# The last layer norm of a 1-core encoder step: three scaling tiles move from ScalarE to GpSimd, and the output leaves in three transfers

## The chip, the cores and the metric

One core of a Trainium2 chip runs the whole program: TensorE (PE), VectorE (DVE), ScalarE (ACT), GpSimd (POOL) and SyncE (SP), which here only issues transfers and waits. The metric is the device time of one execution in microseconds. The kernel before was run three times: 957.76, 958.23 and 964.26, median 958.23 us.

## The reference, cut to what matters

The model is a two-layer hybrid encoder step on 256 prompt frames and 32 sample frames of 1024 features. Each layer is a mixer (RWKV-7, then forgetting attention), a layer norm, a mixture of experts and a second layer norm. The change touches only the very last of these four layer norms, whose result is the output y:

```python
def _layer_norm(z, g, b):
    zf = z.astype(F32)
    mu = jnp.mean(zf, -1, keepdims=True)
    var = jnp.mean(jnp.square(zf - mu), -1, keepdims=True)
    return ((zf - mu) * lax.rsqrt(var + LN_EPS) * g + b).astype(z.dtype)
...
        y = _hmoe(h, p['rg_w'][l], p['rg_b'][l], p['re_w'][l], p['re_b'][l],
                  p['exp_wg'][l], p['exp_wu'][l], p['exp_wd'][l])
        x = _layer_norm(ALPHA * x + gt2 * y, p['ln_g'][l, 1], p['ln_b'][l, 1])
```

## The kernel before, in words

Activations are held feature-major: the 1024 features are KT = 8 tiles of 128 partitions, and the 288 frames (T) lie along the free side, so that one tile is 128x288 float32 and the whole activation 128x2304, 1152 KB. X is the activation that a layer norm writes, Z the one that it reads and changes in place.

A layer norm (n = 0 to 3, the last is n = 3) is written once for each engine, in one function `layer_norm(n)` per engine, and the order on each engine is the order of the code. ACT squares the tiles (L2118) and POOL sums the squares (L2368) while the expert output is still being gathered; PE forms mean and variance (L989 to L996); ACT copies the mean (L2120). Then the mean is taken off: DVE does tiles 0 to 4 (L1617), POOL tiles 5 to 7 (L2373; OWN = 5). DVE works out the inverse of the variance (L1626 to L1628), ACT its root (L2124), DVE multiplies tile after tile by it (L1638, semaphore `u_ready`), and in the odd layer norms ACT follows with one instruction a tile that multiplies by g and adds b (L2128, semaphore `x_ready`). In the even layer norms POOL does that step for X (L2381), after a smaller job on the 32 sample frames of each tile (L2378, semaphore `hs_ready`). In n = 3 POOL has nothing after L2373.

SP, whose queue is in the order of its code, waits for all `x_ready` counts and then issues one transfer of X to the output (L678), waits for it to land, and then for the other outputs, which landed long before. Nothing else follows.

Of the kernel before, what the change touches and what calls it, by code (L numbers as in the profile page):

```python
# [12 lines left out]
ALU = mybir.AluOpType  # L13
# [4 lines left out]
D, KT = 1024, 8  # L18
TP, TS = 256, 32
T = TP + TS  # L20
# [37 lines left out]

MEAN_BANK, BONUS_BANK, VAR_BANK = (1, 2, 5), (6, 3, 4), (7, 0)
H0 = KT  # L60


VEC = {n: i * KT for i, n in enumerate(
# [183 lines left out]
def build(nc, I, O):  # L247
    ctx = ExitStack()
    with ctx:
# [3 lines left out]
        def sem(name):  # L253
            return ctx.enter_context(nc.semaphore(name))
# [31 lines left out]
        def cut(a, n):  # L286
            assert a + n <= ARENA, (a, n, ARENA)
            return arena[:, a:a + n]

        def act_flat(i):  # L290
            return cut(i * ACOL, ACOL)

        def acts(i):
            return act_flat(i).rearrange("p (k t) -> p k t", k=KT)

        A_X, A_H, A_KK, A_XX, A_B = 0, 1, 1, 2, 2
        A_R, A_K, A_V, A_G, A_LD, A_CUM, A_Y, A_A = 3, 4, 5, 6, 7, 8, 9, 10
        X, Hh = acts(A_X), acts(A_H)
# [16 lines left out]
        def v(name, k):  # L315
            return vec[:, VEC[name] + k:VEC[name] + k + 1]
# [6 lines left out]
        def folded(layer, what, k, stream):  # L323
            c = ((layer * 2 + what) * KT + k) * 2 + stream
            return fold[:, c:c + 1]
# [146 lines left out]
        s = {n: sem(n) for n in names}  # L472
# [45 lines left out]
        def _(sp):  # L518
# [155 lines left out]
            half(7, 0)  # L674
            sp.wait_ge(s["ada_done"], ADA_SLOTS)
            moe_loads(1)
            sp.wait_ge(s["x_ready"], 4 * KT)
            sp.dma_start(O["y"], act_flat(A_X)).then_inc(s["out_done"], 16)  # L678
            sp.wait_ge(s["out_done"], 16)
            sp.wait_ge(s["o_over"], 4)  # L680

            sp.wait_ge(s["shift_out"], 16)
# [6 lines left out]
        def _(pe):  # L689
# [10 lines left out]
            def project(mi, rhs_at, ready=None, then=None, first=0):  # L700

                for j in range(first, 2):
                    pe.wait_ge(wready[j], 16 * (mi + 1))
                    for o in range(4):
                        tile = 4 * j + o
                        if mi or tile >= 4:
                            pe.wait_ge(s["tile_free"], mi * 8 + tile - 3)
                        for k in range(KT):
                            if ready and tile == 0:
                                ready(k)  # L710
                            last = mm(ps[:, tile % 4, 0:T], wslot[j][:, k, o * P:(o + 1) * P], rhs_at(k),  # L711
                                      start=k == 0, stop=k == KT - 1)
                        last.then_inc(s["tile_done"], 1)
                        if then:
                            then(tile)
# [283 lines left out]
            def moe(layer):  # L999
# [3 lines left out]
                for k in range(KT):  # L1003
                    pe.wait_ge(s["h_ready"], H0 + 2 * KT * layer + k + 1)
                    pe.wait_ge(s["hs_ready"], KT * layer + k + 1)
# [213 lines left out]
            last.then_inc(s["f_mm"], 1)  # L1219
            pe.wait_ge(s["h_ready"], H0 + 2 * KT)  # L1220
            project(5, lambda k: Hh[:, k, :])
# [764 lines left out]
        def _(act):  # L1986
# [112 lines left out]
            for i in range(KT + 2):  # L2099
# [3 lines left out]
                k = i - 2  # L2103
# [8 lines left out]
            def layer_norm(n):  # L2112
                Z, layer = acts(ZB[n]), n // 2
                if n % 2:
                    act.wait_ge(s["o_over"], n + 1)
                for k in range(KT):
                    act.wait_ge(s["z_ready"], KT * n + k + 1)
                    Ac(acts(SQB[n])[:, k, :], Z[:, k, :], ACT.Square).then_inc(s["ln_sq"], 1)  # L2118
                act.wait_ge(s["ln_mean"], n + 1)
                Ac(lnmu, ps[:, 4, 0:T], ACT.Copy).then_inc(s["ln_mu"], 1)  # L2120
                act.wait_ge(s["ln_mu"], n + 1)
                Ac(lnm2, lnmu, ACT.Square).then_inc(s["ln_m2"], 1)
                act.wait_ge(s["ln_inv"], n + 1)
                Ac(lnr, lnr, ACT.Sqrt).then_inc(s["ln_rstd"], 1)  # L2124
                for k in range(KT):
                    act.wait_ge(s["u_ready"], KT * n + k + 1)
                    if n % 2:
                        Ac(X[:, k, :], Z[:, k, :], ACT.Identity, scale=v(f"g{layer}1", k), bias=v(f"b{layer}1", k))\  # L2128
                            .then_inc(s["x_ready"], 1)
                    else:  # L2130

                        Ac(Hh[:, k, 0:TP], Z[:, k, 0:TP], ACT.Identity, scale=folded(layer, 0, k, 0),
                           bias=folded(layer, 1, k, 0)).then_inc(s["h_ready"], 1)

            def moe(layer):
# [56 lines left out]
                for n in range(2):  # L2192
                    act.wait_ge(s["dn_mm"], layer * NDOWN + NPAIR + n)
                    Ac(ysel[1][:, n * 512:(n + 1) * 512], ps[:, 4 + n, :], ACT.Copy).then_inc(s["y_last"], 1)

            layer_norm(0)
            moe(0)
            layer_norm(1)

            def between(k):  # L2200
# [79 lines left out]
            act.dma_start(O["v"], act_flat(A_VO)).then_inc(s["kv_out"], 16)  # L2280
            act.wait_ge(s["kv_out"], 32)
            layer_norm(2)
            moe(1)
            layer_norm(3)
# [3 lines left out]
        def _(pool):  # L2288
            Pl = nc.gpsimd
# [66 lines left out]
            def layer_norm(n):  # L2356
                Z, Q, layer = acts(ZB[n]), acts(SQB[n]), n // 2
                if n % 2:
                    pool.wait_ge(s["z_in0"], 48 * (layer + 1))
                    for q in range(2):  # L2360
                        c = slice(q * 256, (q + 1) * 256)
                        ch.did(Pl.tensor_tensor(zin[:, 0:2, 0, c], zin[:, 0:2, 0, c], zin[:, 0:2, 1, c], ALU.add))
                        ch.link(Pl.tensor_tensor(zin[0:TS, 2, 0, c], zin[0:TS, 2, 0, c], zin[0:TS, 2, 1, c], ALU.add))
                        pool.sem_inc(s["zsum"], 1)

                for k in range(1, KT - 1):
                    pool.wait_ge(s["ln_sq"], KT * n + k + 1)
                    ch.link(Pl.tensor_tensor(ssum, Q[:, 0, :] if k == 1 else ssum, Q[:, k, :], ALU.add))  # L2368
                pool.sem_inc(s["ln_ssum"], 1)
                pool.wait_ge(s["ln_mu"], n + 1)  # L2370
                pool.wait_ge(s["ln_sq"], KT * (n + 1))
                for k in range(OWN, KT):
                    Pl.tensor_tensor(Z[:, k, :], Z[:, k, :], lnmu, ALU.subtract).then_inc(s["ln_cent"], 1)  # L2373
                if n % 2:
                    return
                for k in range(KT):
                    pool.wait_ge(s["u_ready"], KT * n + k + 1)
                    Pl.tensor_scalar(Hh[:, k, TP:T], Z[:, k, TP:T], folded(layer, 0, k, 1), folded(layer, 1, k, 1),  # L2378
                                     ALU.mult, ALU.add).then_inc(s["hs_ready"], 1)
                for k in range(KT):  # L2380
                    Pl.tensor_scalar(X[:, k, :], Z[:, k, :], v(f"g{layer}0", k), v(f"b{layer}0", k), ALU.mult, ALU.add)\  # L2381
                        .then_inc(s["x_ready"], 1)

            def moe(layer):
# [90 lines left out]
                for b in range(2):  # L2475
                    pool.wait_ge(s[f"o_gath{b}"], (np_ + base) * 16 + 16 * (layer + 1))
                    pool.sem_inc(s["o_over"], 1)

            layer_norm(0)
            moe(0)  # L2480
            layer_norm(1)

            pool.wait_ge(s["ada_done"], 4 * ADA_TURN)
            Pl.dma_start(clf[0:16, :], I["clf"]).then_inc(s["attn_small"], 16)
            for g in range(NGRP):
                if g >= 2:
                    pool.wait_ge(s["att_mm"], APE_TURN.after(g - 2, "SO"))
                for dst, src in ((CK, "ck"), (CV, "cv")):
                    Pl.dma_start(dst[g % 2], I[src][g]).then_inc(s[f"g_in{g % 2}"], 16)
            layer_norm(2)  # L2490
            moe(1)
            layer_norm(3)
# [137 lines left out]
```

## Time and profile before

| | us |
|---|---|
| median of three runs | 958.23 |
| the profiled execution's own time | 957.23 |
| its span, first to last instruction | 955.6 |

| engine | busy in the span |
|---|---|
| PE | 876.6 us, 92% |
| DVE | 368.9 us, 39% |
| ACT | 234.5 us, 25% |
| POOL | 185.4 us, 19% |

The shares are averages over the whole program. The mean granted clock of TensorE was 0.973 of full speed. The profile has a page of groups of instructions, a timeline in order of time (start, duration, engine, line, operation, and in brackets the idle time before it with what ended it), windows with the busy time of each engine and the DMA rate, and the chain of waits that ended last. In a timeline row "x6" after the shapes means that six instructions in a row are merged, and the duration is that of the whole group.

### The profile page before, as it was taken

To read this page: it belongs to the slowest core of one execution; us is meant where nothing else is said; L and a number is where in the kernel's file an instruction comes from. 1 tells how busy PE (TensorE), PEld (TensorE's weight loads), DVE (VectorE), ACT (ScalarE), POOL (GpSimd) and SP (SyncE) were. 2 spreads that over 40 slices of the span, in tenths; PEclk is the share of its full clock that TensorE was granted. 3 is DMA by queue.
4 is the path that set the end of the run, shared out by engine and by line. 5 is a ranking of instruction groups with operands and counts; after the bars stand their busy time and mean duration, and the time that the engine had idled before them with its cause. 6 is when DMAs were issued, how large, how long until landed. Compare 5 with 4: busy or idle time off the path is not lost.

```text
span 955.6 us, 19128 instructions
## 1 busy us (share of the span) xinstructions
PE 876.6 (92%) x8194; PEld 607.2 (64%) x8194; DVE 368.9 (39%) x869; ACT 234.5 (25%) x532; POOL 185.4 (19%) x237
## 2 busy tenths in 40 slices
PE   3899999989989999899988999999999998999873
PEld 0677667869987676655444567756567766554442
DVE  0614332536443647421221606933221374222226
ACT  0312224323322415111100415133232141111004
POOL 0100001203190225412131310000000244221213
PEclk9899999999999999799998999999999998999997
DMA  9947320432045965399999987334736744999941
GB/s 365 415 146 280 124 88 12 152 118 92 21 163 192 374 264 216 131 401 414 399 425 392 381 326 317 117 148 153 263 162 254 312 194 157 408 410 414 425 147 50
DMA packets 29877, 234.64 MB, mean 246 GB/s; under 512 B 6438, under 2 KB 6982, under 8 KB 14656
## 3 DMA queue, kind: packets, MB, share of 16 engines
q1 hardware_dynamic: 20736, 211.50, 55.3%
q0 software_dynamic: 8592, 19.52, 5.4%
q10 hardware_dynamic: 464, 2.39, 0.7%
q8 instruction: 65, 1.06, 0.4%
q14 instruction: 20, 0.16, 0.1%
HBM read 223.36 MB, written 18.94 MB: 254 GB/s over the span
## 4 chain that ended last, share of the span: by engine, by line
PE 76%; DMA 9%; DVE 6%; issue 4%; ACT 2%; POOL 1%; another core or an unknown queue 1%; SPq 0%; POOLq 0%; DVEq 0%; ACTq 0%
PE ps L711 22%; PE ps L1064 9%; PE ps L849 7%; PE ps L1111 5%; PE ps L693 4%; PE ps L856 3%; PE ps L732 3%; PE ps L1261 3%; DMA arena<-in_experts 3%; DMA arena<-in_w 2%; PE ps L1042 2%; PE ps L803 2%; PE ps L862 2%; PE ps L1156 1%; PE ps L774 1%
## 5 line engine op out<-in xcount | busy, mean ns | idle before, releaser
L711 PE MATMUL ps<-arena,ring 128*128 128x288 f32 x832 | 208.8, 411 | 3.8 <-ACT arena L2128 2.0
L711 PEld LDWEIGHTS ps<-arena,ring 128*128 128x128 f32 x832 | 157.4, 191 | 55.0 <-issue 8.7
L1064 PE MATMUL ps<-arena 128*64 128x256 f32 x960 | 118.3, 390 | 14.8 <-DMA arena<-in_experts 8.7
L1064 PEld LDWEIGHTS ps<-arena 128*64 128x64 f32 x960 | 68.0, 139 | 56.1 <-issue 15.1
L693 PEld LDWEIGHTS ps<-con,arena 128*128 128x128 f32 (+2 forms) x350 | 42.6, 148 | 38.0 <-issue 25.5
L849 PE MATMUL ps<-arena 64*64 64x64 f32 x1888 | 61.9, 219 | 5.2 <-issue 3.6
L693 PE MATMUL ps<-con,arena 128*128 128x128 f32 (+2 forms) x350 | 59.4, 302 | 6.7 <-DVE arena L1788 2.8
L849 PEld LDWEIGHTS ps<-arena 64*64 64x64 f32 x1888 | 58.8, 135 | 10.2 <-issue 6.7
L2157 ACT ACTIVATE arena<-ps 128x128 f32<-128x128 f32 x36 | 10.0, 278 | 196.8 <-PE ps L1064 183.5
L1111 PE MATMUL ps<-arena 128*64 128x512 f32 x176 | 51.0, 598 | 0.8 <-DVE arena L1791 0.8
L2021 ACT ACTIVATE arena<-ps 128x288 f32<-128x288 f32 x40 | 16.2, 408 | 121.6 <-PE ps L711 110.2
L2085 ACT ACTIVATE arena<-ps 128x512 f32<-128x512 f32 x44 | 26.2, 596 | 75.6 <-PE ps L849 55.1
L732 PE MATMUL ps<-arena,csil 128*32 128x512 f32 x192 | 26.9, 687 | 17.1 <-DMA arena<-in_w 17.1
L1602 DVE SCALAR_TENSOR_TENSOR arena<-ps,mod,arena 128x256 f32<-128x256 f32 x64 | 20.5, 361 | 52.5 <-PE ps L711 36.8
L1788 DVE TENSOR_TENSOR arena<-arena,ps 128x128 f32<-128x128 f32 x36 | 10.4, 288 | 76.2 <-ACT arena L2157 71.1
L1424 DVE SCALAR_TENSOR_TENSOR arena<-arena,vec 128x288 f32<-128x288 f32 x48 | 21.6, 513 | 42.6 <-PE ps L711 41.6
L1795 DVE TENSOR_SCALAR arena<-ps,TBL 128x512 f32<-128x512 f32 x24 | 16.9, 746 | 47.6 <-PE ps L1111 47.6
L2400 POOL DMA_INDIRECT arena<-hbuf,TBL x16 | 16.7, 1044 | 85.3 <-DVEq L1730 56.9
L1884 DVE SCALAR_TENSOR_TENSOR arena<-arena,csil 128x2048 f32<-128x2048 f32 x14 | 32.9, 2352 | 0.7
L1261 PE MATMUL ps<-arena,ring 128*128 128x288 f32 x128 | 32.7, 409 | 0.0
L2118 ACT ACTIVATE arena<-arena 128x288 f32<-128x288 f32 x32 | 14.2, 443 | 73.3 <-DVEq L1606 66.9
L698 PE MATMUL ps<-con 128*128 128x288 f32 x110 | 31.6, 441 | 0.0
(325 smaller groups left out, 1308.3 us busy)
## 6 DMA issues: line engine op xcount, KB each, us to landing
arena<-in_experts SPq DMA_DIRECT2D x30, 2048.0 KB, 13.2
ring<-in_w SPq DMA_DIRECT2D x24, 2048.0 KB, 8.6
arena<-in_w SPq DMA_DIRECT2D x16, 2048.0 KB, 13.3
arena<-in_experts SPq DMA_DIRECT2D x26, 1024.0 KB, 14.0
ring<-in_experts SPq DMA_DIRECT2D x6, 2048.0 KB, 10.5
ring<-in_experts SPq DMA_DIRECT2D x10, 1024.0 KB, 20.1
zbuf<-arena POOLq DMA_DIRECT2D x2, 2304.0 KB, 17.8
arena<-zbuf SPq DMA_DIRECT2D x8, 512.0 KB, 7.1
```

What stands on the lines that cost most here:

```text
L693: return nc.tensor.transpose(out, in_, ident[0:n, 0:n])
L698: mm(ps[:, bank, 0:T], ident, con[:, 0:T], start=True, stop=True)
L711: last = mm(ps[:, tile % 4, 0:T], wslot[j][:, k, o * P:(o + 1) * P], rhs_at(k), start=k == 0, stop=k == KT - 1)
L732: last = mm(ps[32 * q:32 * q + 32, ADA_BANK[turn], :], c2[:, 2 * j + k, :], w[:, k, q, :], start=j == 0 and k == 0, stop=j == ADA_TURN - 1 ...
L849: last = mm(o, lhs[r, k, :], rhs[r, k, :], start=True, stop=True)
L856: last = mm(ps[r, bank, k * 64:(k + 1) * 64], lhs[r, k, :], rhs[r, k, :], start=n == 0, stop=n == len(terms) - 1)
L1064: last = mm(ps[64 * j:64 * j + 64, 2 + b, 0:256], x(k), ewgu[slot][:, k, j * 256:(j + 1) * 256], start=k == 0, stop=k == KT - 1)
L1111: last = mm(ps[HALF[b], 4 + n, :], hidT[b][:, f * C:(f + 1) * C], ewd[dslot(2 * p + b)][:, f, n * 512:(n + 1) * 512], start=f == 0, stop=f ...
L1261: last = mm(ps[:, b, 0:T], wslot[j][:, k, o * P:(o + 1) * P], X[:, k, :], start=k == 0, stop=k == KT - 1)
L1424: last = V.scalar_tensor_tensor(cut((11 + n % 3) * ACOL + k * T, T), XX[:, k, :], v(f"mu{i}", k), Hh[:, k, :], ALU.mult, ALU.add)
L1884: link(V.scalar_tensor_tensor(turn5[st], w[:, k, :], x, turn5[st], ALU.mult, ALU.add))
L2085: ins = Ac(B[dst], src, ACT.Copy, scale=-1.0 if product == "Bt" else 1.0)
```

## The change

In the last layer norm, tiles 3, 5 and 7 get their multiplication by g and addition of b on POOL instead of ACT. ACT still waits for each tile's `u_ready`, and passes over these three. POOL signals them by `hs_ready`, ACT its five by `x_ready`. SP issues three transfers in place of one: tiles 0 to 2, tiles 3 to 5, tiles 6 and 7, each behind waits for its own tiles, and at the end waits for all three to land. (There are eight tiles; the words "nine tiles" that came with the change do not fit the code.)

```diff
+LAST_POOL = (3, 5, 7)
+LAST_OUT = ((0, 3), (3, 6), (6, 8))
...
             moe_loads(1)
-            sp.wait_ge(s["x_ready"], 4 * KT)
-            sp.dma_start(O["y"], act_flat(A_X)).then_inc(s["out_done"], 16)
-            sp.wait_ge(s["out_done"], 16)
+            for a, b in LAST_OUT:
+                if any(k in LAST_POOL for k in range(a, b)):
+                    sp.wait_ge(s["hs_ready"], 2 * KT + sum(k < b for k in LAST_POOL))
+                sp.wait_ge(s["x_ready"], 3 * KT + sum(k not in LAST_POOL for k in range(b)))
+                sp.dma_start(O["y"][:, a * T:b * T], act_flat(A_X)[:, a * T:b * T]).then_inc(s["out_done"], 16)
+            sp.wait_ge(s["out_done"], 16 * len(LAST_OUT))
...
                 for k in range(KT):
                     act.wait_ge(s["u_ready"], KT * n + k + 1)
+                    if n == 3 and k in LAST_POOL:
+                        continue
                     if n % 2:
                         Ac(X[:, k, :], Z[:, k, :], ACT.Identity, scale=v(f"g{layer}1", k), bias=v(f"b{layer}1", k))\
                             .then_inc(s["x_ready"], 1)
...
                 for k in range(OWN, KT):
                     Pl.tensor_tensor(Z[:, k, :], Z[:, k, :], lnmu, ALU.subtract).then_inc(s["ln_cent"], 1)
+                if n == 3:
+                    for k in LAST_POOL:
+                        pool.wait_ge(s["u_ready"], KT * n + k + 1)
+                        Pl.tensor_scalar(X[:, k, :], Z[:, k, :], v("g11", k), v("b11", k), ALU.mult, ALU.add)\
+                            .then_inc(s["hs_ready"], 1)
                 if n % 2:
                     return
```

On SP, at the end of its queue, before: the readback of the expert output, the one transfer of y, and the waits for the outputs.

```order
L507 DMA arena<-zbuf 128x2x512 [waits z_scat1,z_scat0]
L507 DMA arena<-zbuf 128x2x512
L507 DMA arena<-zbuf 32x2x512
L507 DMA arena<-zbuf 128x2x512 x2
L678 DMA out_y<-arena 128x2304 [waits x_ready]
L249 UNCONDITIONAL_BRANCH [waits st_out,kv_out,shift_out,logf_out,o_over,out_done]
```

The same place in the changed kernel (its line numbers are 3 to 13 higher):

```order
L510 DMA arena<-zbuf 128x2x512 x2
L510 DMA arena<-zbuf 32x2x512
L684 DMA out_y<-arena 128x864 [waits x_ready]
L684 DMA out_y<-arena 128x864 [waits x_ready,hs_ready]
L684 DMA out_y<-arena 128x576 [waits x_ready,hs_ready]
L252 UNCONDITIONAL_BRANCH [waits st_out,kv_out,shift_out,logf_out,o_over,out_done]
```

One transfer of 1152 KB became two of 432 KB and one of 288 KB, in one queue, each behind the waits of its tiles.

On POOL, at the end of its queue, the changed kernel has:

```order
L2376 TENSOR_TENSOR lnw<-arena 128x288 [waits pool_ch,ln_sq]
L2376 TENSOR_TENSOR lnw<-lnw,arena 128x288 [waits ln_sq,pool_ch] x5
L2381 TENSOR_TENSOR arena<-arena,lnw 128x288 [waits pool_ch,ln_sq,ln_mu]
L2381 TENSOR_TENSOR arena<-arena,lnw 128x288 x2
L2385 TENSOR_SCALAR arena<-arena,vec 128x288 [waits u_ready] x3
```

Only the last of these rows is new; the kernel before ends with the subtractions. On ACT the eight instructions of the last step became five: before

```order
L2122 ACTIVATE lnw<-lnw 128x288 [waits ln_mu]
L2124 ACT_TABLE_LOAD
L2124 ACTIVATE lnw<-lnw 128x288 [waits ln_inv]
L2128 ACTIVATE arena<-arena,vec 128x288 [waits u_ready] x8
L249 UNCONDITIONAL_BRANCH
```

and in the changed kernel

```order
L2128 ACTIVATE lnw<-lnw 128x288 [waits ln_mu]
L2130 ACT_TABLE_LOAD
L2130 ACTIVATE lnw<-lnw 128x288 [waits ln_inv]
L2136 ACTIVATE arena<-arena,vec 128x288 [waits u_ready] x5
L252 UNCONDITIONAL_BRANCH [waits u_ready]
```

The instructions of PE and DVE and their waits are the same in both kernels.

## Rows read from the trace of the kernel before

**Rows 1.** Chain of waits that ended last, end of the span: start, us, what.
```profile
939.86 0.77 PE ps L991 x2
...
943.37 1.96 DVE lnw L1628
945.34 0.02 issue
945.36 0.45 ACT lnw L2124
...
947.80 2.18 ACT arena L2128 x4
949.98 0.52 ACTq L249
950.50 0.52 ACT arena L2128
```

**Rows 2.** Timeline, last layer norm, after the root: DVE, ACT and SP.
```profile
946.33 4.69 ACT L2128 ACTIVATE arena<-arena,vec 128x288 f32<-128x288 f32 x8 [0.53 <-DVE arena L1638]
...
947.32 2.29 DVE L1638 TENSOR_TENSOR arena<-arena,lnw 128x288 f32<-128x288 f32 x6
951.04 0.36 SPq L678 DMA_DIRECT2D out_y<-arena  x1
```

**Rows 3.** Timeline of the same stretch in short windows: single instructions of DVE and ACT.
```profile
947.07 0.63 ACT L2128 ACTIVATE arena<-arena,vec 128x288 f32<-128x288 f32 x1
...
947.80 0.63 ACT L2128 ACTIVATE arena<-arena,vec 128x288 f32<-128x288 f32 x1
...
949.16 0.45 DVE L1638 TENSOR_TENSOR arena<-arena,lnw 128x288 f32<-128x288 f32 x1
```

**Rows 4.** Windows: start:end, length, engines, PE clock, DMA share, GB/s.
```profile
951.00:952.00 1.00, 0.00 (x0) 0.00 (x0) 0.00 (x0) 0.02 (x1) 0.00 (x0) 0.50 0.28 120
952.00:953.00 1.00, 0.00 (x0) 0.00 (x0) 0.00 (x0) 0.00 (x0) 0.00 (x0) 0.50 0.98 415
953.00:954.00 1.00, 0.00 (x0) 0.00 (x0) 0.00 (x0) 0.00 (x0) 0.00 (x0) 0.50 0.97 406
954.00:955.00 1.00, 0.00 (x0) 0.00 (x0) 0.00 (x0) 0.00 (x0) 0.00 (x0) 0.50 0.57 240
```

**Rows 5.** DMA issues: what, queue, count, KB each, us from issue to landing.
```profile
hbuf<-arena SPq DMA_DIRECT2D x4, 512.0 KB, 2.8
...
out_y<-arena SPq DMA_DIRECT2D x1, 1152.0 KB, 4.1
...
out_swkv<-ring POOLq DMA_DIRECT2D x1, 256.0 KB, 3.3
...
hbuf<-arena SPq DMA_DIRECT2D x2, 128.0 KB, 2.4
```

**Rows 6.** Timeline, first layer norm: POOL beside DVE's multiplications.
```profile
363.57 0.46 DVE L1638 TENSOR_TENSOR arena<-arena,lnw 128x288 f32<-128x288 f32 x1 [0.20 <-ACT lnw L2124]
...
364.14 5.03 POOL L2378 TENSOR_SCALAR arena<-arena,fold 128x32 f32<-128x32 f32 x8 [2.42 <-DVE arena L1638]
365.05 2.31 DVE L1638 TENSOR_TENSOR arena<-arena,lnw 128x288 f32<-128x288 f32 x6
365.20 1.12 POOL L2378 TENSOR_SCALAR arena<-arena,fold 128x32 f32<-128x32 f32 x1
366.30 1.14 POOL L2378 TENSOR_SCALAR arena<-arena,fold 128x32 f32<-128x32 f32 x1
...
368.80 0.37 POOL L2378 TENSOR_SCALAR arena<-arena,fold 128x32 f32<-128x32 f32 x1
369.14 4.54 POOL L2381 TENSOR_SCALAR arena<-arena,vec 128x288 f32<-128x288 f32 x8
```

**Rows 7.** Timeline, last layer norm: DVE and POOL both take off the mean.
```profile
941.14 2.85 POOL L2373 TENSOR_TENSOR arena<-arena,lnw 128x288 f32<-128x288 f32 x3 [1.86 <-ACT lnw L2120]
941.47 1.05 DVE L1617 TENSOR_TENSOR arena<-arena,lnw 128x288 f32<-128x288 f32 x1
...
945.24 0.40 DVE L1617 TENSOR_TENSOR arena<-arena,lnw 128x288 f32<-128x288 f32 x1
```

**Rows 8.** What SP's queue waited for in the last 56 us.
```profile
SPq L249 <- DMA out_y<-arena: 3.6, 1, 3.6
```

## The prediction

> **What bounds the kernel now.** The program as a whole is bound by TensorE, but the change touches only what comes after TensorE's last instruction, so I read the end of the span and nothing else. First the chain of waits [rows 1]: TensorE's last link in it, the mean, starts at 939.86; after that the chain runs through the inverse (DVE), the root (ACT), and ACT's L2128, one instruction a tile. Then the timeline of that stretch [rows 2]: ACT's eight instructions fill 946.33 to 951.02 without a gap, and SP issues the output transfer at 951.04. Last the DMA views: the transfer lands 4.1 us after its issue [rows 5], at 955.14, and SP does nothing but wait for it [rows 8]; the span closes 0.46 later, at 955.6. So 4.6 of the 955.6 us lie behind the last computed tile, and everything that the change can reach is the 9.3 us from 946.33 on. That alone limits the answer: 1% of the time is 9.6 us, and I take 1% as about what a measurement of this kernel can tell from no change.
>
> Who limits whom in the last step: DVE finishes a tile every 0.37 us ((949.16 - 947.32) / 5 [rows 2, 3]), while ACT, once it no longer waits, needs 0.52 (in rows 1, 2.18 for four is 0.54, and the last two are 0.52 each). ACT's first three start at 946.33, 947.07 and 947.80 [rows 2, 3], each just after DVE's tile. DVE's tiles are then done at about 947.77 (tile 2), 948.14 (3), 948.50 (4), 948.87 (5), 949.24 (6) and 949.61 (7): each start plus 0.45. ACT ends 1.41 us after DVE. A second engine beside ACT can win back at most that.
>
> **Part 1, tiles 3, 5 and 7 on POOL.** ACT's own queue gets shorter: tile 4 can start at 948.53 and tile 6 at 949.27, each 0.63 long, so ACT is done at 949.90. The end is then POOL's. The same instruction on POOL (L2381, 128x288, two column operands) took 4.54 us for eight with DVE idle, 0.57 each [rows 6]. POOL starts 0.11 after DVE's tile (DVE's first multiplication of the first layer norm ends at 363.57 + 0.46 = 364.03, and POOL starts at 364.14 [rows 6]). With nothing in the way tile 3 runs 948.25 to 948.82, tile 5 948.98 to 949.55, and tile 7 949.72 to 950.29. This is the low end for the last tile: 950.3, 0.7 earlier than now.
>
> It will not be that, because DVE is multiplying at the same time, and the trace has that very meeting. In the first layer norm POOL's L2378, only 32 columns wide, took 1.12 and 1.14 us while DVE ran the same stream L1638, and 0.37 once DVE had stopped, while DVE's six took 2.31 against 2.29 without POOL beside them [rows 6, 2]. So POOL loses about 0.75 us an instruction there and DVE nothing. In the other meeting, both taking off the mean, it was DVE that lost: its second subtraction took 1.05 against 0.40 [rows 7], 0.65 lost to a POOL instruction of 288 columns. The new instruction has the width of the second case and the kind, partner and timing of the first; I go by the first, and let DVE lose what the wider instruction is longer, 0.57 - 0.37 = 0.20, once. Then tile 3 runs from 948.25 for 0.57 + 0.75 = 1.32 to 949.57; DVE ends tile 7 at 949.81; tile 5 waits out those 0.24 and takes 0.57, to 950.38; tile 7 follows, to **950.95**. That is where ACT ends now (951.02). I cost this part at nothing, and its cover is exact: of the 1.41 us that ACT lags, all goes to POOL's waits. High end: DVE loses 0.65 to each of the two POOL instructions ahead of its last tile (949.61 + 1.30 = 950.91) and POOL's last still takes 1.32 and 0.11, 952.34.
>
> A rule speaks here. The Trainium skill, page "SBUF — State Buffer" (section "SBUF: two separate sides"), has the port pair that DVE and GpSimd share as an exclusive lock, taken for the whole instruction by whichever starts first when DVE has two SBUF inputs; the other fully blocks. Rows 7 agree; rows 6 agree only for POOL, as DVE there lost 0.02 in six. What the lock would do if it held in full here is the second rival.
>
> **Part 2, three transfers.** Tiles 0 to 2 are done by ACT at 947.80 + 0.63 = 948.43; their 432 KB are issued then. The windows give the transfer of now as 120 GB/s in its first window and 415, 406 and 240 after [rows 4]: data flow from about 951.71 (0.29 of that window at 415) to 954.58, 0.67 after the issue, 2.87 for 1.18 MB, and 0.56 to landing. By that the first 432 KB flow from 949.1 to 950.2, fully beside computation. Tiles 3 to 5 are complete with tile 5 at 950.38; their data flow 951.1 to 952.2. The last 288 KB are issued at 950.97, could flow from 951.7, stand behind the second for 0.5, take 0.72 to 952.9 and land at 953.5. Adding all three issues (0.36 each on SP) costs nothing: they are more than 0.5 apart and SP has no other work.
>
> Rows of whole transfers of that size bound it: from issue to landing 2.4 us at 128 KB and 2.8 at 512 KB, both SBUF to memory on SP's queue, 3.3 for 256 KB on POOL's queue [rows 5], and 0.67 + 0.72 + 0.56 = 1.95 by the windows for 288 KB with nothing ahead. I take 2.4: between 1.95 and the 2.57 that lies between the two SP rows, which were taken while weights were loading, where here the queue is empty but for the second transfer. That gives a landing at 950.97 + 2.4 = **953.4** instead of 955.14: **1.7 us less**. Keeping the ends: 1.95 to 3.3.
>
> The Trainium skill, page "DMA: Bandwidth & Descriptors" (section "Anatomy of one DMA — SWDGE (gpsimd) path", a fit for transfers from GpSimd's queue), gives about 2.0 us fixed plus the bytes at 436 GB/s; an estimate by that is 4.7 for the whole and 2.7 for 288 KB, so a gain of 2.0 if both are taken from the page. Its 4.7 is above the 4.1 of the row, so the row decides.
>
> **The sum.** Last tile 951.02 to 950.95 (-0.07), transfer 4.1 to 2.4 (-1.7), nothing elsewhere since no instruction ahead of 948 us is touched. The span goes from 955.6 to 953.9 and the profiled execution's 957.23 to 955.5. The median of runs stands 1.0 above the profiled execution, so 958.23 - 1.7 = **956.5**.
>
> **The rivals.**
> (a) POOL is not held up. Against it are rows 6; for it, that only five short DVE instructions remain when POOL starts. The last tile is at 950.3; the gain is 0.7 + 1.7 = 2.4 and, with the transfer at 1.95, up to 2.9. Time 955.8. Chance 0.15.
> (b) The lock holds both ways. POOL's tile 3 waits for DVE's tile 4 (948.50), then holds DVE for 0.57; DVE ends tile 5 at 949.52 and, having the next one queued, tile 6 at 949.89; POOL's tile 5 takes 0.57 and DVE's tile 7 comes at 950.9, POOL's at 951.6. The last tile is 0.6 later than now, the gain 1.1, the time 957.1. For it: rows 7; against: rows 6. Chance 0.25. This is the rule of the Trainium skill's page "SBUF — State Buffer", same section.
> (c) The split doesn't do what it says: POOL's tile 5 ends so close to tile 7 that the second and third transfers leave together. Their 720 KB take 1.76 at the rate of rows 4, so 950.97 + 0.67 + 1.76 + 0.56 = 954.0. The gain is 1.2, the time 957.0. Tiles 5 and 7 are only 0.57 apart in my own sum, so this is near. Chance 0.12.
> (d) Slower: POOL's last tile comes so late that it eats the whole transfer gain. Its place is the POOL instruction of tile 7; with a transfer of 2.4 it decides from an end at 952.7 on, which is 1.7 us past ACT's end now. The high end of part 1 (952.34) doesn't reach it alone; with the 3.3 of the row on POOL's queue it lands at 955.66, 0.5 us later than now, 958.7. That needs both worst rows at once. Chance 0.05.
>
> **Chances and range.** My forecast has the remaining 0.43. All cases lie between 2.9 us less and 0.5 more, 955.3 to 958.7. The runs shown are 957.76, 958.23 and 964.26, so a median moves by half a microsecond easily and by more if two of three are high; I widen the range to 954.4 to 959.4 for that. Faster by over 1% would need more than the whole 9.3 us stretch: 0.01 for what I don't see. Slower by over 1% can't come from these rows, only from scatter like the run of 964.26: 0.01. Within 1%: 0.98.
>
> **What would show it.** In the profile after: three out_y transfers, the first issued near 948.5, the last near 951.0, landing 2.4 later; ACT's last L2136 ending near 949.9, 1.1 earlier than now; the three new POOL instructions at 1.3, 0.8 and 0.6 us (0.6 each speaks for (a)); DVE's last multiplication ending between 949.6 and 949.8 (950.9 speaks for (b)). The second and third issue less than 0.4 apart speak for (c). I would be wrong if the end were set by something other than the landing of the last transfer, or if anything ahead of 946 us moved by more than tenths.

## The result: slower, by a close that the prediction did not have

Over 19 runs of each, the changed kernel's median was 966.73 us and the one before had 961.36; the ratio is 1.0066 with a 95% interval of 1.0043 to 1.0088. A few executions of either kernel are longer at a lower granted clock; the ratios leave them out, the medians are of all runs. I had forecast 956.5 (954.4 to 959.4) from a median of 958.23: a gain of 1.7 us. The time is outside the range, on the other side. The difference is under 1%, but the sign is wrong, and the profile says why.

The measure that I use from here on is the **tail**: from the start of DVE's first multiplication in the last layer norm to the end of the span. What lies ahead of it wanders by several microseconds from run to run, the tail does not. It is 955.57 - 945.84 = 9.74 us in the kernel before and 961.82 - 949.17 = 12.65 us in the changed one: 2.9 us longer.

The timeline of the changed kernel after the root (start, duration, engine, line, operation; DVE, ACT, POOL and SP), which answers to [rows 2]:

```profile
949.17 0.46 DVE L1644 TENSOR_TENSOR arena<-arena,lnw 128x288 f32<-128x288 f32 x1 [0.20 <-ACT lnw L2130]
...
949.66 2.10 ACT L2136 ACTIVATE arena<-arena,vec 128x288 f32<-128x288 f32 x3 [0.53 <-DVE arena L1644]
...
950.65 2.29 DVE L1644 TENSOR_TENSOR arena<-arena,lnw 128x288 f32<-128x288 f32 x6
951.58 2.96 POOL L2385 TENSOR_SCALAR arena<-arena,vec 128x288 f32<-128x288 f32 x3 [4.26 <-DVE arena L1644]
951.79 3.11 SPq L684 DMA_DIRECT2D out_y<-arena  x3
951.93 1.36 ACT L2136 ACTIVATE arena<-arena,vec 128x288 f32<-128x288 f32 x2 [0.17 <-DVE arena L1644]
```

and two short windows of it, with single instructions:

```profile
951.58 1.82 POOL L2385 TENSOR_SCALAR arena<-arena,vec 128x288 f32<-128x288 f32 x1 [4.26 <-DVE arena L1644]
...
953.40 1.14 POOL L2385 TENSOR_SCALAR arena<-arena,vec 128x288 f32<-128x288 f32 x2
...
954.56 0.33 SPq L684 DMA_DIRECT2D out_y<-arena  x1
```

Its output transfers (KB each, us from issue to landing), which answer to [rows 5]:

```profile
out_y<-arena SPq DMA_DIRECT2D x2, 432.0 KB, 2.4
out_y<-arena SPq DMA_DIRECT2D x1, 288.0 KB, 2.6
```

Up to here all is nearly as forecast. The last tile is done at 954.54, 5.37 us into the tail (ACT's last before: 951.02 - 945.84 = 5.18), the last transfer is issued at 954.56 and lands at 957.15, 7.98 into the tail, where the one transfer of before landed at 9.32. But the span does not close 0.4 us later, as it did then. It runs on to 961.8. What SP's queue waited for (us in total, times, longest), which answers to [rows 8]:

```profile
SPq L252 <- PEq L252: 4.4, 1, 4.4
SPq L252 <- DMA out_y<-arena: 2.1, 1, 2.1
```

The same view of the kernel before has the row "PEq L249" with 0.2 us. L249 and L252 are the close of the program, where every engine waits for every other; the name in that row is that of an engine of the close, not of the culprit. The instructions of that line say more (duration in ns three times, then the start). Before:

```profile
L249 PEldq DRAIN  x1: 1298/1298/1298, 940.3 to 940.3; - x1
L249 POOLq DRAIN  x1: 9925/9925/9925, 941.1 to 941.1; - x1
L249 DVEq DRAIN  x1: 2211/2211/2211, 947.5 to 947.5; - x1
L249 ACTq DRAIN  x1: 1402/1402/1402, 949.6 to 949.6; - x1
...
L249 SPq DRAIN  x1: 7/7/7, 955.4 to 955.4; - x1
```

Changed:

```profile
L252 POOLq EVENT_SEMAPHORE  x2: 17/17/17, 961.6 to 961.7; - x2
L252 PEldq DRAIN  x1: 1297/1297/1297, 943.7 to 943.7; - x1
L252 DVEq DRAIN  x1: 2211/2211/2211, 950.8 to 950.8; - x1
...
L252 POOLq DRAIN  x1: 8595/8595/8595, 953.0 to 953.0; - x1
```

Each engine ends with a drain. Those of PE, DVE and ACT are over within 0.05 us of that engine's last instruction (DVE: 950.78 + 2.21 = 952.99 against 952.94). GpSimd's is not. Before it was over at 941.11 + 9.93 = 951.03, and GpSimd's last subtraction had ended at 941.14 + 2.85 = 943.99 [rows 7]: **7.04 us** later. That was hidden, with 4.3 us to spare, under the wait for the output. In the changed kernel GpSimd's last instruction is the third tile, at 954.54, and the drain is over at 952.99 + 8.60 = 961.58, again 7.04 later, and 4.2 us after SP had come to its own drain at 957.35. The first row there, GpSimd's semaphore at 961.6, is what lets the others go: theirs come at 961.8.

### The profile page after: what moved, and what is told of

Its sections match the earlier page's. It is cut to its first block, busy times and chain, and to the rows that moved or that the text cites. A ratio compares the mean times of both kernels' runs of the same rounds, so it can differ in the third digit from the quotient of the medians.

```text
span 961.8 us, 19135 instructions
## 1 busy us (share of the span) xinstructions
PE 875.0 (91%) x8194; PEld 603.5 (63%) x8194; DVE 369.6 (38%) x869; ACT 232.9 (24%) x529; POOL 188.2 (20%) x240
## 4 chain that ended last, share of the span: by engine, by line
PE 73%; DMA 9%; DVE 6%; issue 5%; POOL 2%; ACT 2%; another core or an unknown queue 1%; SPq 0%; POOLq 0%; DVEq 0%; ACTq 0%
PE ps L717 21%; PE ps L1070 8%; PE ps L855 7%; PE ps L1117 5%; PE ps L862 3%; PE ps L699 3%; PE ps L738 3%; PE ps L1267 3%; DMA arena<-in_w 2%; DMA zbuf<-arena,IDXS 2%; DMA IDXJ<-tbl 2%; DMA arena<-zbuf 2%; PE ps L1048 2%; PE ps L809 2%; PE ps L868 2%
## 5 line engine op out<-in xcount | busy, mean ns | idle before, releaser
L699 PEld LDWEIGHTS ps<-con,arena 128*128 128x128 f32 (+2 forms) x350 | 40.2, 141 | 38.9 <-issue 26.3
L699 PE MATMUL ps<-con,arena 128*128 128x128 f32 (+2 forms) x350 | 56.9, 291 | 7.2 <-DVE arena L1794 2.8
L1797 DVE COPY arena<-ps 128x128 f32<-128x128 f32 x36 | 10.5, 292 | 55.5 <-PE ps L699 44.6
```

The costliest lines, as they stand in the source:

```text
L699: return nc.tensor.transpose(out, in_, ident[0:n, 0:n])
```

## Experiments

Each starts from the kernel named. In the table the tail and the points in it are worked out from the trace as above, all from the start of DVE's first multiplication in the last layer norm; "behind it" is how long after GpSimd's last instruction its drain was over.

| kernel | GpSimd's last instruction ends | its drain over | behind it | last landing | tail | ratio to before, 95% |
|---|---|---|---|---|---|---|
| before | -1.85 | 5.20 | 7.04 | 9.32 | 9.74 | |
| changed | 5.37 | 12.41 | 7.04 | 7.98 | 12.65 | 1.0066 (1.0043 to 1.0088) |
| e1_split | -1.85 | 5.19 | 7.04 | 7.33 | 7.75 | 0.9949 (0.9909 to 0.9989) |
| e2_pool | 5.36 | 12.40 | 7.04 | 9.50 | 12.64 | 1.0069 (1.0039 to 1.0098) |
| e3_touch | 3.94 | 10.96 | 7.03 | 9.33 | 11.20 | |
| e4_dve | -1.85 | 5.20 | 7.05 | 7.33 | 7.75 | 0.9975 (0.9936 to 1.0014) |
| n1_same | -1.85 | 5.20 | 7.04 | 9.33 | 9.75 | 0.9962 (0.9927 to 0.9997) |
| n2_again | 5.37 | 12.41 | 7.04 | 7.99 | 12.65 | 1.0015 (0.9985 to 1.0046) |
| e5_drains | -1.85 | -1.79 | 0.07 | 9.33 | 9.75 | |
| e6_four | -1.85 | 5.20 | 7.04 | 6.95 | 7.37 | |
| e7_drained | 5.37 | 5.45 | 0.08 | 7.98 | 8.40 | 1.0008 (0.9974 to 1.0041) |
| e8_half | -1.85 | 1.02 | 2.87 | 9.33 | 9.75 | |
| e9_four | -1.85 | 5.19 | 7.04 | 6.96 | 7.38 | 0.9970 (0.9931 to 1.0009) |

### e1_split: the three transfers alone

```diff
-LAST_POOL = (3, 5, 7)
+LAST_POOL = ()
```

> The changed kernel's three transfers alone; all eight tiles are scaled by ACT as in the kernel before. I call tail the time from the start of DVE's first multiplication of the last layer norm (L1638 in the kernel before) to the end of the span: 9.7 us before (945.84 to 955.57), 12.6 in the changed kernel (949.17 to 961.82). Theory (closing drain): the trace of the changed kernel has a DRAIN on GpSimd that ends 7.04 us after its last instruction (954.54 to 961.58), as in the kernel before (943.99 to 951.03), and all engines wait for it; the transfers themselves gain as forecast. It expects here: GpSimd's drain over by 5.2 us into the tail, the last transfer issued at 5.2, landed 2.4 to 2.6 later, tail 8.1 to 8.3, time 1.4 to 1.6 us less than the kernel before. Rival (split): several small transfers at the end delay the close; it expects a tail near 12.6. Rival (layout): the changed code moves something ahead of the last layer norm by some 3 us, as the medians differ by 5.4 and the tails by only 2.9; if the transfers' code does it, this kernel is some 1.5 to 2 us slower than the kernel before in all although its tail is shorter.

Measured: tail 7.75 us, 2.0 less than before. The split gains, and by more than I had forecast: with ACT's tiles the second transfer is issued at 4.17 instead of 4.83, so the last one finds the way nearly free and lands 2.1 us after its issue instead of 2.6. The rival "split" falls. The whole runs came out at 0.9949 (0.9909 to 0.9989), 4.9 us less, more than the tail explains; if the transfers' code moved something to later, as the rival "layout" has it, they would be 1.5 to 2 us slower, so for this part it falls too.

### e2_pool: the three tiles on GpSimd alone

```diff
-LAST_OUT = ((0, 3), (3, 6), (6, 8))
+LAST_OUT = ((0, 8),)
```

> The changed kernel's three tiles on GpSimd alone, with one transfer of the whole output as before. Closing drain: GpSimd's last instruction ends 5.4 us into the tail, its drain 7.0 later, tail 12.6 to 12.7, as long as in the changed kernel, although the one transfer lands at 9.5; time 2.9 us more than the kernel before. Split: tail about 9.9, since there is no split. Layout: 2.9 us more than the kernel before if nothing else moves, about 6 if GpSimd's added code moves something earlier.

Measured: tail 12.64, as in the changed kernel, though the transfer landed at 9.50. SP waited 2.9 us for the close here, 4.4 in the changed kernel, both up to the same moment: whatever the transfers win is lost to the drain. The whole loss in the tail belongs to the tiles on GpSimd. The whole runs came out at 1.0069, 6.6 us more (3.8 to 9.4). That is above the 2.9 of the tail, and it is what the rival "layout" expected (about 6), if GpSimd's added code moves something earlier in the program; n1_same and n2_again below take this up.

### e3_touch: one small instruction more on GpSimd, from the kernel before

```diff
+                if n == 3:
+                    pool.wait_ge(s["u_ready"], KT * n + KT)
+                    Pl.memset(small[:, 7:8], 0)
```

> The kernel before with one instruction more on GpSimd: it waits for DVE's last multiplication and then sets one unused column (128x1). No tile moves, the transfer is one. Closing drain: the instruction ends some 4.1 to 4.3 us into the tail, the drain 7.04 later, tail 11.4 to 11.6 instead of 9.7, with nothing else changed. If the drain's length hangs on the work just done (three tiles of 288 columns), it is shorter after this one, and the tail stays at 9.7. If what counts is the port contention of GpSimd with DVE, nothing changes: 9.7.

Measured: tail 11.20, 1.5 more than before, for an instruction of 0.1 us (the expectation was 0.2 to 0.4 higher, as I had put the instruction's end at 4.1 to 4.3 and it came at 3.94). It had 6 runs, too few for a ratio. Its row in the timeline, and the one of its closing drain:

```profile
952.81 0.10 POOL L2376 MEMSET small<- 128x1 f32 x1 [5.69 <-DVE arena L1638]
```

```profile
L249 POOLq DRAIN  x1: 7143/7143/7143, 952.8 to 952.8; - x1
```

The drain is over 7.03 us behind it, whether the last work is three tiles or one column. It is not contention with DVE either, which had just finished.

### e4_dve: three transfers, tiles 6 and 7 on DVE

```diff
+LAST_DVE = (6, 7)
+LAST_OUT = ((0, 3), (3, 6), (6, 8))
...
+                if n == 3:
+                    for k in LAST_DVE:
+                        dve.wait_ge(s["u_ready"], KT * n + k + 1)
+                        V.tensor_scalar(X[:, k, :], Z[:, k, :], v("g11", k), v("b11", k), ALU.mult, ALU.add)\
+                            .then_inc(s["hs_ready"], 1)
...
+                    if n == 3 and k in LAST_DVE:
+                        continue
```

(on the kernel before; SP's transfers, left out here, are those of the changed kernel with LAST_DVE in place of LAST_POOL)

> The three transfers as in the changed kernel, and tiles 6 and 7 scaled by DVE instead of ACT, after its multiplications; GpSimd ends as in the kernel before. Closing drain: GpSimd's drain is over at 5.2 in the tail and hidden. DVE's tile 7 is scaled 4.5 us into the tail (3.77 for the last multiplication, then two instructions of 0.42), the last transfer lands 2.5 later, tail 7.4 to 7.6, time 2.1 to 2.3 us less than the kernel before. Split: tail near 12. Had it been the engine that is added to the last step, whichever it is, that closes late, it would be above 9.7 too.

Measured: tail 7.75, the same as e1_split and 0.15 above what I expected. Here, adding DVE to the last step does no harm. But it brings nothing with these transfers: the last issue came at 4.64 instead of 5.21, and it then took 2.7 us instead of 2.1, behind the second transfer. In e1_split, here and in the changed kernel alike the last one lands 0.71 to 0.72 us after the second, so issuing it earlier gains nothing unless the second lands earlier too.

### n1_same and n2_again: each kernel once more

The kernel before and the changed kernel, with no edit.

> The kernel before, unchanged, timed against itself, to learn what the measurement makes of no change. All theories: ratio within 0.4% of 1. The changed kernel is 0.66% slower (6.3 us) and GpSimd's tiles alone 0.69%, where the closing drain accounts for 2.9 us, 0.3%. If the same kernel comes out 0.2% or more off, the rest of about 3.4 us may be the measurement; if it is within 0.1%, some of the rest is likely real and lies ahead of the last layer norm (layout).

> The changed kernel, unchanged, timed once more. Closing drain alone: ratio 1.003, tail 12.6 us again. Layout on top of it: ratio 1.006 to 1.007 again, with the start of DVE's first multiplication of the last layer norm some 3 us later than in the kernel before run beside it.

Measured: the kernel before against itself came out at 0.9962, an interval that just leaves out 1, and the changed kernel at 1.0015 instead of 1.0066. Their medians, 963.65 and 961.46, are 2.2 us apart, their ratios 0.5%, some 5 us; the 2.9 of the tails lies between. So two ratios of one kernel differ by 0.4 to 0.5% for no cause in the code. The traces show where executions differ: DVE's first multiplication of the last layer norm started at 945.8 and 953.9 in two traces of the kernel before, and at 949.2 and 946.1 in two of the changed one. The tails were 9.74 and 9.75, and 12.65 and 12.65. The rest of the first ratio, 6.3 - 2.9 = 3.4 us, is of the size of that scatter. The ratio of e2_pool has the same excess, 6.6 - 2.9 = 3.7 us. Over all 13 traces of this document that first multiplication started at 946.1 to 955.4 in the four kernels with tiles on GpSimd (mean 950.4) and at 945.8 to 957.2 in the other nine (mean 951.6): no shift shows, but one of 3 us would hide in such a spread. That something ahead of the last layer norm moved is not shown, and not excluded.

### e5_drains: drains on GpSimd through the whole program

```diff
+            pool.drain()
             Pl.dma_start(ENT[:], I["ent"]).then_inc(s["tbl_fill"], 16)
             for layer in range(2):
                 Pl.dma_start(tbl[layer], I["tbl0"]).then_inc(s["tbl_fill"], 16)
+            pool.drain()
...
             layer_norm(0)
+            pool.drain()
             moe(0)
             layer_norm(1)
+            pool.drain()
...
             moe(1)
+            pool.drain()
+            pool.drain()
             layer_norm(3)
```

(on the kernel before; two more stand behind the 16 small operations and behind the transfer of the state)

> The kernel before with explicit drains on GpSimd at eight places: before its first transfer, after its three first transfers, after its 16 small operations at the start, before the first jobs of the recurrence (two more transfers behind it), after layer norm 0, after layer norm 1, and two in a row ahead of layer norm 3; the closing one comes as ever. Length counted from the end of the instruction before it. If every drain on GpSimd behind computation costs 7 us, the six later ones take 7.0 each and the second of the pair as well or near nothing, when there is nothing left to wait for. If the length comes from the indirect transfers of the expert stage, the drains ahead of it are short (0.2, as the one at the very start of the program, 0.47 to 0.64) and the ones after it 7. If it is the fetch of code at the close, none of the explicit ones is long. Tail: 9.7, as the kernel before.

Measured, with the number of transfers that GpSimd had issued since the drain before, and how long after GpSimd's last work ahead of it each drain was over:

| place | transfers since the last drain | us behind the work ahead of it |
|---|---|---|
| before any transfer | 0 | 0.04 (the drain itself) |
| behind the first three, in flight | 3 | 8.3, about when they land |
| behind 16 small operations | 0 | 0.07 |
| behind three more, the last in flight | 3 | 2.4 |
| after layer norm 0 | 2 | 0.24 |
| after layer norm 1, behind the expert stage | 34 | 2.87 |
| ahead of layer norm 3, behind the second one | 43 | 3.58 (the drain itself; GpSimd's last work had ended 9 us before it) |
| once more at once | 0 | 0.05 (the drain itself) |
| the close | 0 | 0.07 |

The rows behind layer norm 1 (the drain, and the work ahead of it, which ends at 537.73 + 2.88 = 540.61; the drain is over at 543.47), for the pair and for the close:

```profile
L2487 POOLq DRAIN  x1: 5783/5783/5783, 537.7 to 537.7; - x1
```

```profile
537.73 2.88 POOL L2377 TENSOR_TENSOR arena<-arena,lnw 128x288 f32<-128x288 f32 x3 [1.87 <-ACT lnw L2120]
```

```profile
L2498 POOLq DRAIN  x1: 3577/3577/3577, 911.7 to 911.7; - x1
```

```profile
L2499 POOLq DRAIN  x1: 46/46/46, 915.3 to 915.3; - x1
```

```profile
L249 POOLq DRAIN  x1: 2942/2942/2942, 943.5 to 943.5; - x1
```

The last one began with the subtractions (2.84 us from 943.52) and was over 0.07 us behind them. None of my three readings was quite right: not every drain costs 7, and it is neither the close nor indirect transfers alone. 2.87 / 34 and 3.58 / 43 are 0.084 and 0.083 us, and 85 transfers (33 direct, 52 indirect), all that GpSimd issues in the program, make 7.04 / 85 = 0.083. This led to the theory of e7 and e8: **a drain on GpSimd pays about 0.083 us for each transfer issued from its queue since the last drain, also where these landed hundreds of microseconds ago.** It is not the time since the last drain nor the other work since then: ahead of the drain after layer norm 0 lie 215 us, 76 computing instructions and 2 transfers, and it costs 0.24; ahead of the next one 168 us, 15 computing instructions and 34 transfers, and it costs 2.87. With the 0.07 of an empty drain taken apart, 0.07 + 0.082 for each transfer gives every row with nothing in flight to within 0.03, the 0.24 for two included.

### e6_four and e9_four: four transfers, two tiles on DVE

```diff
-LAST_OUT = ((0, 3), (3, 6), (6, 8))
+LAST_OUT = ((0, 2), (2, 4), (4, 6), (6, 8))
```

(against e4_dve; the two are the same kernel, with one run of e6_four and twelve of e9_four)

> Tiles 6 and 7 on DVE as in the run before of that kind, and four transfers of two tiles (288 KB) in place of three. There the last transfer was issued at 4.64 us into the tail and took 2.7 to land, 0.6 longer than the 2.1 of the last one with ACT's tiles, as it stood behind the second of 432 KB. With four, the third is issued at 4.2 and carries 288 KB, and the last lands at 4.64 + 0.67 + 0.72 + 0.56 = 6.6 to 6.9, tail 7.2 to 7.4 against 7.75. If the three issues of 0.35 us in a row on SP hold it back, it stays at 7.75. GpSimd's drain is over at 5.2 in all theories.

> The version that should beat both kernels: tiles 6 and 7 on DVE, four transfers of two tiles, GpSimd as in the kernel before. Its single look gave a tail of 7.37 against 9.74 before, so 2.4 us less, ratio about 0.9975. The same kernel against itself came out at 0.9962 with an interval of 0.35% on each side, so I expect a ratio between 0.994 and 1.001 and take the tail in its trace as the measure: 7.4 again.

Measured: tail 7.37 and 7.38, 2.4 us less than the kernel before and the shortest of all. The last transfer lands at 6.95. The DMA rows of the second:

```profile
out_y<-arena SPq DMA_DIRECT2D x4, 288.0 KB, 2.1
```

Its ratio, 0.9970, agrees with 2.4 us (0.9975) and its interval holds 1; with the scatter above, whole runs do not show so small a gain. By the tails it beats both kernels. Four transfers with ACT alone were not run; an estimate from e1_split's last issue at 5.21 and the 2.08 us that the first 288 KB took here, with nothing ahead, is a landing at 7.29 or later, against 6.95. So the gain over e1_split needs both, the earlier tiles and the smaller transfers.

### e7_drained: the changed kernel with one drain in a wait

```diff
             moe(1)
+            pool.drain()
             layer_norm(3)
```

> The changed kernel with one explicit drain on GpSimd, ahead of layer norm 3, where it waits some 16 us for the readback of the expert output. Theory (the closing drain works off GpSimd's 85 transfers, some 0.08 us each, however long ago they landed): the explicit drain takes 7.0 inside that wait, the closing one 0.07 behind the last of the three tiles, which still end 5.4 us into the tail; the last transfer lands at 8.0 as in the changed kernel, and now sets the end: tail 8.4 against 12.65 (changed) and 9.74 (before), ratio about 0.9986. Rival (late computation on GpSimd makes the close long, not its transfers): tail 12.6 again.

Measured, the explicit drain and the close:

```profile
L2505 POOLq DRAIN  x1: 7018/7018/7018, 917.3 to 917.3; - x1
```

```profile
L252 POOLq DRAIN  x1: 1627/1627/1627, 959.2 to 959.2; - x1
```

```profile
957.83 2.96 POOL L2385 TENSOR_SCALAR arena<-arena,vec 128x288 f32<-128x288 f32 x3 [4.25 <-DVE arena L1644]
958.04 3.11 SPq L684 DMA_DIRECT2D out_y<-arena  x3
```

```profile
SPq L252 <- DMA out_y<-arena: 2.1, 1, 2.1
...
SPq L252 <- PEq L252: 0.2, 1, 0.2
```

The 7.02 us now lie in GpSimd's wait for the readback. The three tiles are as long as before (2.96), the close is over 0.08 us behind them, SP's wait for it falls from 4.4 to 0.2, and the tail is 8.40, as expected to the hundredth. With the drain paid elsewhere, the change does most of what I had forecast for it: 1.34 us less than the kernel before in the tail, of 1.7. The late computation on GpSimd was never the cost; the rival falls. The ratio of whole runs, 1.0008, can't tell 1.3 us from nothing.

### e8_half: one drain between the two halves, from the kernel before

```diff
             layer_norm(2)
+            pool.drain()
             moe(1)
```

> The kernel before with one explicit drain on GpSimd between layer norm 2 and the second expert stage. If a drain costs by the transfers since the last one, the explicit one has 51 behind it (25 direct, 26 indirect) and takes 4.1 to 4.4 us, the closing one has the second stage's 34 (8 direct, 26 indirect) and takes 2.9, as the one behind the first stage's did, instead of 7.04. If it is a fixed cost that any earlier drain takes away, the closing one takes 0.07. Tail 9.7.

Measured:

```profile
L2491 POOLq DRAIN  x1: 10097/10097/10097, 774.6 to 774.6; - x1
```

```profile
775.96 4.52 POOL L2381 TENSOR_SCALAR arena<-arena,vec 128x288 f32<-128x288 f32 x8
```

The drain is over at 784.74, 4.27 us behind the work, for 51 transfers (0.084 each); the closing one 2.87 behind, for 34. The row of the closing one (GpSimd's last work ends at 948.83, the drain at 951.69):

```profile
L249 POOLq DRAIN  x1: 5742/5742/5742, 946.0 to 946.0; - x1
```

Those 34 cost the same here as behind the first expert stage. Both drains have 26 indirect transfers to pay for; the difference of the two, 17 direct ones for 1.40 us, is 0.082 each. That leaves 2.87 - 8 x 0.082 = 2.21 us for the 26, or 0.085 each with the 0.07 of an empty drain counted in, so direct and indirect ones cost alike. That excludes a fixed cost that any earlier drain takes away.

## Why the prediction was wrong, by its own steps

- **What bounds the kernel.** I read the chain, the timeline up to the transfer and SP's wait, and wrote that SP "does nothing but wait" for the landing and that everything behind the last tile is that wait. This was true of the kernel before, and it was here that I stopped too soon: the close was in the trace, with GpSimd's drain of 9925 ns at its line, and I did not ask for that line. "Nothing else follows", in my description of SP's queue, has the same gap: the close follows. The question that was missing is which engine would be last if the landing came earlier, or if its own last instruction came later.
- **Part 1, tiles on GpSimd: the step that failed.** I "cost this part at nothing", with ACT's lag as cover. The tiles themselves came close: the last one ended 5.37 into the tail where 950.95 - 945.84 = 5.11 was forecast. The term left out is GpSimd's drain, 7.04 us behind its last instruction, which moving work to GpSimd after DVE's multiplications carried from 5.20 to 12.41 in the tail. It alone is 12.65 - 8.40 = 4.25 us, by e7 against the changed kernel.
- **Port contention.** I let rows 6 decide, and they were right in kind. GpSimd's first tile took 1.82 us, not 1.32: it began at 951.58, DVE's stream ended at 952.94, and the tile 0.46 us after that, so it was held up nearly to the end of the stream. DVE lost nothing (2.29 for six, as before; forecast 0.20). The next two took 0.57 each. For rival (b), DVE would have had to stand still, and the full lock of the Trainium skill's page "SBUF — State Buffer", section "SBUF: two separate sides", would have done that to it; the trace has only GpSimd's half of it.
- **Part 2, three transfers: right in kind, and slightly mis-sized.** Forecast: 2.4 us from the last issue to landing, measured 2.6 in the changed kernel and 2.1 in e1_split. The first transfer left where it should (2.62 into the tail, just behind ACT's tile 2) and lay wholly beside computation. In the landing alone the change gained 9.32 - 7.98 = 1.34 us against the 1.7 forecast; the last issue came 0.27 later than forecast (5.40 for 5.13) and its transfer took 0.19 more. All of it was under the drain.
- **The rivals.** None was this. (c) did not happen by its own sign: the second and third issues were 0.57 apart, not less than 0.4. What it is about, the last transfer behind the second, did cost some 0.5 us: 2.59 against 2.08 for 288 KB with nothing ahead (the first transfer of e6_four). (Its 720 KB would take 1.79 us at the rate of rows 4, not 1.76; its time stays.) (d) had the right place, GpSimd's tile 7, and the wrong price: it asked when that tile would be late enough to delay the transfer, from an end 1.7 us past ACT's on, and not what GpSimd itself still had to do once done. With the drain the point from which it decides is quite another: the close comes 0.24 after the drain (12.65 - 12.41), so GpSimd's last instruction has to end by 9.74 - 7.04 - 0.24 = 2.46 us into the tail, and tile 3, the first of the three, only starts at 2.41. By this estimate one of them would have been too many; no run tried one alone.
- **What would show it.** I had written that the prediction fails if the end is set by something other than the landing of the last transfer. That is what happened.
- **The size.** The tail explains 2.9 us of the first ratio's 6.3 (4.1 to 8.5). The second timing gave 1.0015, less than the tail alone would, but e2_pool again gave 1.0069, and the same kernel came out at 0.9962 against itself. Whether the rest is scatter or something ahead of the last layer norm stays open. My range allowed for the scatter of one set of runs, not for the shift between sets: the kernel before had medians of 958.23, 961.36, 962.08, 963.69 and 965.62, the last three on three different chips.

## What to carry to other kernels

The span ends when the last engine has closed, not when the output has landed: before giving an engine late work, look at the last line of the program for each engine's drain and write down how long after its last instruction it is over. GpSimd owes time at its next drain for every transfer that it has issued since the last one, so its last instruction has to stand that much ahead of the end, or the debt has to be paid with an explicit drain in some earlier wait (e7: 7.0 us moved into a wait of 16, closing drain 0.08). For the last step of this kernel the better helper is the engine whose own drain is short: DVE, with the output in four parts, gives a tail of 7.4 us against 9.7.

## What the runs showed of the hardware that I had not expected

- GpSimd's drain takes 0.082 to 0.084 us for each transfer issued from its queue since the last drain: 7.04 us for 85, 4.27 for 51, 3.58 for 43, 2.87 for 34, and 0.04 to 0.08 for none, equal for direct and indirect ones, and long after they landed. Behind transfers still in flight it lasts until just after their landing (8.3 us behind the first three, over 0.17 us after the last of them landed). Why a transfer that landed long ago still costs time is not shown.
- The Trainium skill, page "VectorE: DVE Perf Modes", section "The DRAIN you can't avoid", has the drains that the runtime puts before and behind a program as constant at about 12 ns on all five engines. The drains read here stand at lines of the program and need not be those. At its start they take 7 to 10 ns on four engines and 169 ns on GpSimd; at its close 7 ns on SP, 1.3 to 2.2 us on PE, DVE and ACT, each over within 0.05 us of the engine's last work, and 9.9 us on GpSimd, 7.04 of it behind its last work. So that figure is no guide to the close.
- A GpSimd instruction of 288 columns that meets DVE's stream of instructions with two operands in SBUF waits for nearly all of it (1.82 us against 0.57), and DVE is not slowed (2.29 us for six either way). In [rows 7] it was DVE that lost 0.65. Which of the two loses was not studied further.
- Transfers in one queue, close behind one another, share the rate: the last 288 KB landed 2.1 us after its issue with the second 1.04 us ahead of it (e1_split), 2.6 with it 0.57 ahead (changed), and 2.7 with it 0.46 ahead (e4_dve). In each of the three it landed 0.71 to 0.72 us after the second.
